# Moving the activation tiles of a two-block transformer kernel to other SBUF byte offsets against its weight tiles

## The reference, cut to what matters

```python
hn = _rmsnorm(h, norm_g[i])
u = hn @ w_in[i]                                   # 2048 x 5632
h = h + jnp.concatenate([ya, yb], axis=-1) @ w_out[i]
e = _rmsnorm(p[i] @ w_pe[i], pe_g[i])              # 256 x 2048: the embedding
h = h + e * jax.nn.sigmoid(h @ w_pg[i])
...
p = h @ fox_w_in[j]                                # second block, first layer
x = x + y @ w_out
```

## Time and profile before

| | |
|---|---|
| median of 3 runs | 1772.52 us (1771.68 to 1772.86) |
| the profiled execution's own time | 1763.33 us |
| its span, first to last instruction | 1761.5 us |
| TensorE busy, of the span | 99% |
| VectorE, ScalarE busy | 74%, 51% |
| granted TensorE clock, mean | 0.999 of full speed |
| instructions | 35797 |

### The profile page before, as it was taken

The page is one execution under the profiler, slowest core; times in us unless marked ns, Lnnn a source line. Parts: engine busy times, 40 slices in busy tenths (PEclk is TensorE's granted clock), DMA queues, the critical chain, the costliest instruction groups (busy, mean ns, idle before and its releaser), DMA issues.

```text
span 1761.5 us, 35797 instructions
## 1 busy us (share of the span) xinstructions
PE 1742.4 (99%) x14393; PEld 1673.6 (95%) x14393; DVE 1307.6 (74%) x2087; ACT 901.2 (51%) x1326; POOL 37.6 (2%) x48
## 2 busy tenths in 40 slices
PE   8999999999999999999999999999999999999997
PEld 7999999999999999999999899998989999999886
DVE  7899889986779988999677765656555666677754
ACT  5433664545544355556465464545455553665553
POOL 0000000000000000000000110000100000000000
PEclk9999999999999999999999999999999999999999
DMA  7566555565656665456556666655655556555553
GB/s 234 183 213 198 185 145 170 188 199 193 199 180 211 191 202 150 151 184 211 187 191 197 199 192 195 197 183 169 212 166 180 192 180 186 164 160 175 171 191 131
DMA packets 200082, 326.07 MB, mean 185 GB/s; under 512 B 14911, under 2 KB 66319, under 8 KB 199821
## 3 DMA queue, kind: packets, MB, share of 16 engines
q1 hardware_dynamic: 197085, 320.85, 58.5%
q10 hardware_dynamic: 2864, 3.36, 0.6%
HBM read 320.42 MB, written 2.69 MB: 183 GB/s over the span
## 4 chain that ended last, share of the span: by engine, by line
PE 91%; DVE 7%; ACT 1%; issue 0%; DMA 0%; DVEq 0%; ACTq 0%
PE g L495 72%; PE g L506 11%; DVE cacc L1155 3%; DVE w_lo L909 3%; PE att L605 2%; PE att L650 2%; PE att L629 2%; ACT w_hi L1538 0%; PE att L495 0%; PE att L799 0%; PE att L559 0%; DMA cacc<-in_norm_g_dram 0%; DVE glu L1127 0%; PE att L869 0%; DVE glu L1118 0%
## 5 line engine op out<-in xcount | busy, mean ns | idle before, releaser
L909 DVE TENSOR_TENSOR w_lo<-stage,w_hi 128x1024 fp32r<-128x1024 f32 x577 | 703.4, 1227 | 371.3 <-ACT w_hi L1538 370.4
L1538 ACT CAST w_hi<-stage 128x1024 fp32r<-128x1024 f32 x577 | 599.8, 1051 | 607.7 <-PE g L495 414.9
L495 PE MATMUL g<-a_hi,w_hi 128*128 128x256 f32 x2496 | 700.8, 281 | 2.1 <-DVE w_lo L909 1.4
L495 PE MATMUL g<-a_lo,w_hi 128*128 128x256 f32 x2496 | 692.7, 278 | 0.0
L495 PE MATMUL g<-a_hi,w_lo 128*128 128x256 f32 x2496 | 692.6, 277 | 0.0
L495 PEld LDWEIGHTS g<-a_hi,w_hi 128*128 128x128 f32 x2496 | 470.7, 189 | 10.3 <-issue 8.1
L495 PEld LDWEIGHTS g<-a_lo,w_hi 128*128 128x128 f32 x2496 | 470.6, 189 | 0.0
L495 PEld LDWEIGHTS g<-a_hi,w_lo 128*128 128x128 f32 x2496 | 470.0, 188 | 0.2
L495 PE MATMUL g<-b_hi,w_hi 128*128 128x256 f32 x1440 | 401.7, 279 | 0.8 <-DVE w_lo L909 0.7
L495 PE MATMUL g<-b_lo,w_hi 128*128 128x256 f32 x1440 | 398.7, 277 | 0.0
L495 PE MATMUL g<-b_hi,w_lo 128*128 128x256 f32 x1440 | 398.7, 277 | 0.0
(11 more groups left out here) (232 smaller groups left out, 1373.6 us busy)
## 6 DMA issues: line engine op xcount, KB each, us to landing
stage<-in_fox_w_in_dram SPq DMA_DIRECT2D x128, 512.0 KB, 3.8
stage<-in_w_in_dram SPq DMA_DIRECT2D x112, 512.0 KB, 3.8
stage<-in_swa_w_in_dram SPq DMA_DIRECT2D x72, 512.0 KB, 3.9
stage<-in_w_in_dram SPq DMA_DIRECT2D x128, 256.0 KB, 3.1
stage<-in_w_out_dram SPq DMA_DIRECT2D x64, 512.0 KB, 4.2
stage<-in_w_pg_dram SPq DMA_DIRECT2D x64, 512.0 KB, 4.1
stage<-in_fox_w_out_dram SPq DMA_DIRECT2D x32, 512.0 KB, 4.5
stage<-in_swa_w_out_dram SPq DMA_DIRECT2D x32, 512.0 KB, 3.9
```

The costliest lines, as they stand in the source:

```text
L495: mm = pe.matmul(acc[:, j * S:(j + 1) * S], w[:, slot, c0 + j * P:c0 + (j + 1) * P], xx[:, k, :], start=st and m == 0 and j % 2 == 0, stop ...
L909: dve.tensor_tensor(w_lo[:, slot, :], stage[:, slot, :], w_hi[:, slot, :].bitcast(F32), ALU.subtract).then_inc(*t.inc("w_split"))
L1538: act.copy(w_hi[:, slot, :], stage[:, slot, :]).then_inc(*t.inc("w_rounded"))
```

## The change

Two sizes of the unused space are set. `APART` goes from 240 to 80 floats, and a second unused tile of 96 floats goes between `a_lo` and `b_hi`. With the same laying out, the first pair (`a_hi`, `a_lo`) starts 320 bytes behind a multiple of 512 from the weights, 192 below them modulo 512; the second pair (`b_hi`, `b_lo`) and the tiles from `h` to `glu` start 704 behind, 192 above; `cacc`, `pe_hi` and `pe_lo` start 128 above. No instruction, wait, order or size of a working tile changes.

```diff
-APART = 240
+APART = 80
+APART2 = 96
...
         sb("apart", [APART])
         a_hi = sb("a_hi", [KT, S], F32R)
         a_lo = sb("a_lo", [KT, S], F32R)
+        sb("apart2", [APART2])
         b_hi = sb("b_hi", [KT, S], F32R)
         b_lo = sb("b_lo", [KT, S], F32R)
```

## The result

The changed kernel takes 1788.29 us (1787.82 to 1790.05, 4 runs) against 1772.68 us (1771.68 to 1772.86, 4 runs) for the kernel before: a ratio of 1.0091, 95% interval 1.0079 to 1.0103. It is 15.6 us slower; the forecast was 50 us slower, 1822. The measured time lies in the stated range of 1760 to 1845.

The account below looks back on a forecast made before the run. TensorE's matmul pace, mainly line 495, was taken as the bound. 43.1 + 12.8 - 5.9 = 50.0 us on the 1772.52 us median gave 1822.5, rounded to 1822 us; range 1760 to 1845.

Parts of the forecast that it names:

- The bound: TensorE, 91% of the chain, line 495 alone 72%: time is the number of matmuls times their pace.
- the direction: Slower as summed, since the only other offset in the trace is slower; chance 0.57, own range 1780 to 1845 us.
- 128 below as the near end of a slope: Embedding's place in line 495, 283 against 277.25 ns a record, taken as nearest guide to the new places.
- The first part: Line 495 with the `a` pair, 64 to 192 below: 7488 matmuls at 5.75 ns more, 43.1 us.
- The second part: Line 495 with the `b` pair, 64 below to 192 above: 4320 matmuls, 12.8 us between ends 4.8 and 24.8.
- Line 506 and the embedding at nothing: Line 506, ends 4.3 us either way, and the embedding's 192 matmuls, -1.3 to 0 us: both taken as 0.
- The room in the waits: First block's convolution: TensorE's waits for `w_lo` in line 495 absorb slower matmuls, 5.9 us off.
- The extra is per matmul and comes on top of either: The 50.0 us add equally to the profiled execution, 1763.33 us, or the median 9.2 us above it, 1772.52.
- No change: Rival: pace hangs on how a stream restarts, not on place; 1772.5 us within 3.5; chance 0.13.
- a pace holds until the next break: Line 495's streams: either pace, once entered after a break in the stream, lasts until the next break.
- The faster rival: Line 495: far enough from the weights only the 113.35 ns pace is left; 1762.5 us; chance 0.30.
- Its far end: Even 113.35 ns holds a stall; line 495 falls to the transposes' 109 ns, 51 us less, 1721 us.

Follow-up runs that it names:

- The five profiles above: Profiled executions with both pairs at 64 or 80 below or 192 above, the kernel before twice among them: 1763.3, 1762.2, 1768.1, 1767.6 and 1772.8 us.
- the 25 later runs: Kernel before, no edit, timed in the follow-up session beside its own repeat: 1764.04 us (1761.99 to 1772.11).

## Why the prediction was right or wrong

**The bound: right; the direction: in part by luck.** Time follows the pace of line 495's matmuls at a full clock; the distance of the tiles moves the pace; nothing else changed. But slower was argued from 128 below as the near end of a slope, and there is none. The first pair went to a worse place, the second to one as good as its old one; by the prediction's reason both would have been worse.

**The first part: the term that was mis-sized.** "The nearest is 128 below, at 64 bytes' distance and on the same side" priced 192 below by the embedding's rows, 5.75 ns a matmul, 43.1 us. Measured: 2.99 ns, 21.7 us. At the embedding's place the pairs do pay nearly that much, 4.4 ns (118.64 against 114.28), as the kernel with both pairs at 128 below shows. The step that failed is the carrying over to 192: there is no slope on which 192 is a neighbour of 128. Places repeat every 256 bytes, 192 below is 64 above, and most streams there run at the slower of the two paces already in the earlier trace rows. Looking back, 117.7 against 114.3 ns over 7488 matmuls would have been 25.5 us; no row of the kernel before said that this pace was the one to take.

**The second part: mis-sized for the same reason.** 12.8 us were summed, 4.9 us came, and none of it is a price of the place: 192 above is 64 below, and moving the second pair alone changes nothing (ratio 1.0003). Of the 4.9 us some 4.3 are two stretches of the second pair, 768 and 192 matmuls, that follow the first without a break and run at its pace; the rest are short stretches that start after a break, some quick before and slow now and one the other way. The weighting by distance round the 512 had no ground.

**Line 506 and the embedding at nothing:** 1.3 us and under 0.1 us, within the ends given. **The room in the waits:** 5.9 us were taken off; 2.8 came off, of which the waits for `w_lo` show 1.2.

**"The extra is per matmul and comes on top of either": wrong.** The five profiles above say that the 9.2 us between the profiled execution and the median before were long streams, quick in the one and slow in the others; the runs near 1772 themselves have no profile. In the changed kernel's profile these are slow already, so its profiled execution (1788.4 us) and its median (1788.29) agree. The errors add up: 21.4 for the first part, 7.9 for the second, 9.3 for this, less 1.3 for line 506 and 3.1 for the waits, make the 34.2 us from 1822.5 to 1788.3.

By this reading the 15.6 us are the change against runs that had the slow long streams. From profile to profile, both pieces quick before, it is 25.1 us. Against the median of the 25 later runs, 1764.0, the same 1788.3 would be 24.3 us, and the like kernel with the first pair moved alone measured 1.0129 in that session. How often the kernel before is near 1772 differs: 4 of 4 runs beside the changed kernel, 3 of 25 in the next session, 3 of 5 in another, none of 11 in a third. What sets this is open.

**The rivals.** No change falls as a forecast, but its premise, that a pace can hang on how a stream begins, holds in part: that is the spread of the kernel before and the second pair's 4.9 us. The prediction's own sentence that a pace holds until the next break is too strong: where the moving tile changes place the pace can change in the midst of a stream (the piece of 1068 with the first pair moved alone). The Trainium skill ("TensorE: Matmul & The Clock Gate", Part 2, step by step) gives the moving operand and the loading of weights a read port each, so that neither takes bandwidth from the other. With the same instructions the time went from 1763 to 1819 us by the distance of the tiles alone; the runs do not agree with the rule as far as these streams go, though which reads meet was not found. The faster rival named the two paces rightly and had the sign wrong: the first pair's new place keeps mostly the slow one. Its far end, 109 ns, was seen in no stream of line 495 in any run.

## What to carry to other kernels

Where matmuls bound the time, read the pace of each stream from start to start, and try the distance between the stationary and the moving tiles in steps of 32 bytes over 256: here the worst place that was tried, 0, where tiles with no space between them would lie, takes 1.0286 times the kernel before (1.0211 to 1.0361), some 50 us. Price a new place by a row of the same place modulo the period, and where no row has it, measure before weighting neighbours. One profile can show a stream at another pace than the timed runs had, so look at several before adding its time to a median.

## What the runs showed of the hardware that was not expected

- The pace of fp32r matmuls of 256 columns with a load of weights each depends on the distance between the two tiles with a period of 256 bytes and in classes of 32: 113.35 or 117.8 ns at 64 and 80 below, the same two but mostly 117.8 at 64 above, 118.3 at 32 and 48 below, 117.3 or 118.7 at 96 below, 118.7 at 128 below (120.0 too, with the embedding), 120.0 at 0.
- At one place two paces are stable. A stream enters one after a break and can keep it for more than 1000 matmuls, also over a change of the moving tile; where the new tile lies at another place, the pace can change there without a break. At 64 below many streams change from the slow to the quick pace in their first few matmuls; in the first pair of the changed kernel none does.
- What decides the pace at a break, and which reads meet, is open. Distances that are no multiple of 16 bytes were not tried, and the period of 256 is shown by 192 above being as 64 below, and 192 below as 64 above.
